# A linear recurrent unit whose three products go by the seven-product scheme, and whose sqrt(1 - a^2) is made without a reciprocal

## The reference, cut to what matters

```python
h = rms_norm(x, mix_norm[0])
u = h @ w_in                                   # [512, 1024] @ [1024, 2048]
gate_branch, x_branch = jnp.split(u, 2, axis=-1)
gate_branch = jax.nn.gelu(gate_branch)
xc = causal_depthwise_conv(x_branch, conv_w, conv_b)        # width 4
r = sigmoid(xb @ w_r + b_r); i = sigmoid(xb @ w_i + b_i)    # 16 blocks of 64 x 64
log_a = 8.0 * r * log_sigmoid(lam)
a = exp(log_a)
bt = sqrt(-expm1(2.0 * log_a)) * (i * xc)
hs[t] = a[t] * hs[t - 1] + bt[t]               # scan over the tokens
x = x + (gate_branch * hs) @ w_out             # @ [1024, 1024]
```

## Time and profile before

| | us |
|---|---|
| median of 3 runs | 3106.22 (3105.04 to 3106.98) |
| the profiled execution | 3106.63 |
| its span, first to last instruction | 3104.9 |
| TensorE busy | 3003.0 (97%) |
| VectorE busy | 1768.4 (57%) |
| ScalarE busy | 649.4 (21%) |
| Pool busy | 412.3 (13%) |
| recurrent unit, first product matmul to the MLP's first | 34.15 to 228.50 |

### The profile page before, as it was taken

How to read it: one execution, slowest core, us unless ns; L and a number is a source line. 1 busy time by engine, 2 the same in 40 slices (tenths; PEclk the granted TensorE clock), 3 DMA queues, 4 the chain that set the end, 5 groups by cost and what they waited for, 6 DMA issues and landing times.

```text
span 3104.9 us, 42252 instructions
## 1 busy us (share of the span) xinstructions
PE 3003.0 (97%) x18102; PEld 2554.3 (82%) x18102; DVE 1768.4 (57%) x2317; ACT 649.4 (21%) x1184; POOL 412.3 (13%) x390
## 2 busy tenths in 40 slices
PE   6989999999899999989989999999999999999998
PEld 5878888888678888878778878888888777888887
DVE  4646645455454653531566668887556134877754
ACT  1311100021341110002336531221010164111201
POOL 2112210120001220020013301111120011111101
PEclk9999999999999999999999999999999999999999
DMA  4222231322102222212100022223222100222320
GB/s 120 68 66 83 82 109 55 96 69 68 41 14 83 94 82 77 87 56 69 61 1 4 4 91 82 82 82 102 75 82 82 55 1 19 68 92 94 102 75 28
DMA packets 207574, 209.50 MB, mean 67 GB/s; under 512 B 8996, under 2 KB 206332, under 8 KB 207388
## 3 DMA queue, kind: packets, MB, share of 16 engines
q1 hardware_dynamic: 207356, 206.76, 20.9%
q10 hardware_dynamic: 32, 0.03, 0.0%
HBM read 204.65 MB, written 2.10 MB: 67 GB/s over the span
## 4 chain that ended last, share of the span: by engine, by line
PE 91%; DVE 5%; ACT 2%; issue 1%; POOL 1%; SPq 1%; DMA 0%; POOLq 0%; DVEq 0%; ACTq 0%
PE pp L252 55%; PE pp L149 16%; PE pp L1179 4%; PE pp L2626 2%; PE pp L2606 1%; PE pp L1915 1%; PE pp L1284 1%; PE pp L1898 1%; PE pp L1574 1%; PE pp L1870 1%; PE pp L2655 1%; PE pp L1307 1%; PE pp L2278 1%; DVE arena L328 1%; DVE arena L1015 1%
## 5 line engine op out<-in xcount | busy, mean ns | idle before, releaser
L252 PE MATMUL pp<-arena 128*128 128x264 f32 (+1 forms) x8176 | 1800.6, 383 | 5.9 <-DVE arena L309 4.1
L252 PEld LDWEIGHTS pp<-arena 128*128 128x128 f32 x8176 | 1550.3, 190 | 254.8 <-DVE arena L309 5.5
L149 PE MATMUL pp<-arena 128*128 128x256 f32 (+5 forms) x2400 | 536.4, 384 | 10.7 <-DVE arena L1025 8.0
L149 PEld LDWEIGHTS pp<-arena 128*128 128x128 f32 (+4 forms) x2400 | 447.2, 187 | 96.0 <-issue 15.6
L810 POOL TENSOR_TENSOR sq<-sq 128x512 f32<-128x512 f32 (+1 forms) x48 | 80.6, 1680 | 741.9 <-ACT sq L790 739.0
L340 ACT COPY arena<-pp 128x528 f32<-128x528 f32 (+1 forms) x58 | 33.6, 580 | 584.4 <-PE pp L252 539.4
L328 DVE TENSOR_TENSOR arena<-arena 128x256 f32<-128x256 f32 (+4 forms) x172 | 145.6, 869 | 6.0 <-POOL arena L2507 2.4
L2433 ACT ACTIVATE arena<-arena,par 128x528 f32<-128x528 f32 x88 | 68.1, 821 | 385.8 <-DVE arena L2464 385.8
L2507 POOL TENSOR_TENSOR arena<-arena 128x528 f32<-128x528 f32 x44 | 72.1, 1638 | 494.5 <-DVE arena L2476 494.5
L1149 POOL TENSOR_TENSOR arena<-arena 128x1024 f32<-128x1024 f32 x32 | 83.4, 2607 | 324.8 <-ACT arena L1097 281.6
L1179 PE MATMUL pp<-arena 128*128 128x256 f32 (+1 forms) x576 | 125.7, 380 | 0.0
(11 more groups left out here) (290 smaller groups left out, 2830.1 us busy)
## 6 DMA issues: line engine op xcount, KB each, us to landing
arena<-in_mlp_w_dram SPq DMA_DIRECT2D x64, 1024.0 KB, 5.5
arena<-in_ffn_up_dram SPq DMA_DIRECT2D x44, 1024.0 KB, 5.1
arena<-in_ffn_down_dram SPq DMA_DIRECT2D x16, 1408.0 KB, 8.0
arena<-in_fox_w_in_dram SPq DMA_DIRECT2D x12, 1024.0 KB, 5.5
arena<-in_lru_w_in_dram SPq DMA_DIRECT2D x8, 1024.0 KB, 7.0
arena<-in_lru_w_out_dram SPq DMA_DIRECT2D x4, 1024.0 KB, 5.2
arena<-in_fox_w_out_dram SPq DMA_DIRECT2D x4, 1024.0 KB, 5.3
arena<-in_rw_wk_dram SPq DMA_DIRECT2D x4, 1024.0 KB, 7.6
```

Source lines behind the costliest of these rows:

```text
L149: mm = pe.matmul(bank[0:m, h, 0:r.shape[1]], slot[0:kp, kk, j * P:j * P + m], r, start=kt == 0, stop=kt == nk - 1)
L252: return pe.matmul(k.pp[seventh(k, name, n, i) % NB][:, j, 0:hw], stationary[i][:, kk, j * P:(j + 1) * P], moving[i][:, kk, :], start=kk = ...
```

## The change

Three things, all in `stage_lru`:

1. The x, gate and output products use `plan_seven` and `product_seven`. VectorE gets their weight sums, input sums and `combine`; ScalarE gets six `keep_first` copies. `first_sums` of the x product is run by the stage ahead (`stage_scale`, now with `late=True`, which moves the root of the norm behind the first copy). For x and gate, `combine` stores through `stored`: one add out of PSUM and one multiply by `rs` for each output quarter of two tiles.
2. 1 - a^2 is tanh(-log a) times (1 + a^2). ScalarE makes a^2 with a second exponential (scale `c16`) into xc, once Pool has read xc; VectorE does one fused operation, `root_square`. The add and the reciprocal go.
3. The order on VectorE is new, since outputs now come in groups of four tiles: convolutions 0 to 3 behind the first pair of the x product, 4 to 7 behind the second; scans 0 to 3 behind the first pair of the gate product, 4 to 7 behind the second; then y with the output product's input sums.

The semaphores of weight and input sums are shared by all stages with counting bases (`Steps`, `weight_steps`, `input_steps`), which changes no order.

```diff
-    plan_product(k, "lru_x", w_in, [(D, 2 * D)], "dve")
+    norm = plan_seven(k, "lru_x", w_in, [(D + c1, D + c2) for c1, c2 in PAIRS])
     k.psum.add("lru_ri", ["act"] * (2 * KT))
-    plan_product(k, "lru_gate", w_in, [(0, D)], "dve")
-    plan_product(k, "lru_out", w_out, [(0, D)], "dve")
+    plan_seven(k, "lru_gate", w_in, PAIRS)
+    plan_seven(k, "lru_out", w_out, [(2 * n * GW + GW, 2 * n * GW) for n in range(2)])
...
+    def first_sums(e):
+        e.wait_ge(k.h_ready, hb + KT)
+        weight_sums(e, k, "lru_x", 0, Sx, xsum_s, "a21")
+        input_sums(e, X, T_, 0, KH, hw, hin_s, 0, (0, 1))
+        weight_sums(e, k, "lru_x", 0, Sx, xsum_s, "s2")
+        weight_sums(e, k, "lru_x", 0, Sx, xsum_s, 1)
+        input_sums(e, X, T_, 0, KH, hw, hin_s, 0, (2, 3))
...
     def act(e):
+        keep_first(e, k, "lru_x", 0, tx, hw)
+        root(e, k, norm)
...
         for f in range(KT):
             e.activation(T[:, f, :], r[:, f, :], ACT.Tanh, scale=nc8[:, f:f + 1]).then_inc(ta, 1)
-            e.wait_ge(ta, 2 * f + 1)
+            e.wait_ge(ix_s, f + 1)
+            e.activation(xc[:, f, :], r[:, f, :], ACT.Exp, scale=c16[:, f:f + 1]).then_inc(ta, 1)
+            e.wait_ge(ta, 3 * f + 2)
             e.activation(r[:, f, :], r[:, f, :], ACT.Exp, scale=c8[:, f:f + 1]).then_inc(ta, 1)
+        was_read(e, k, seventh(k, "lru_x", 1, THREE))
+        e.wait_ge(conv, KT)
+        keep_first(e, k, "lru_gate", 0, to, hw)
         for f in range(KT):
+            if f == KT // 2:
+                keep_first(e, k, "lru_gate", 1, to, hw)
             e.wait_ge(m2_s, f + 1)
             e.activation(T[:, f, :], T[:, f, :], ACT.Sqrt).then_inc(ms_s, 1)
...
     def dve(e):
...
+        for n in range(2):
+            add = stored(lambda f, half: xb[:, f:f + 2, 3 + half * hw:3 + (half + 1) * hw], n, x_s)
+            combine(e, k, "lru_x", n, tx, ux, hw, add,
+                    middle=(lambda e: weight_sums(e, k, "lru_x", 1, Sx, xsum_s, 0)) if n == 0 else None)
+            if n == 0:
+                weight_sums(e, k, "lru_x", 1, Sx, xsum_s, 1)
+            for f in range(4 * n, 4 * n + 4):
+                convolve(f)
...
+        for f in range(4):
+            root_square(f)
+        combine(e, k, "lru_gate", 0, to, uo, hw, stored(gate_at, 0, g_s),
+                middle=lambda e: weight_sums(e, k, "lru_gate", 1, S_, gsum_s, 0))
+        weight_sums(e, k, "lru_gate", 1, S_, gsum_s, 1)
+        for f in range(4, KT):
+            root_square(f)
+        for f in range(4):
+            scan(f)
+        combine(e, k, "lru_gate", 1, to, uo, hw, stored(gate_at, 1, g_s))
+        for f in range(4, KT):
+            scan(f)
         for f in range(KT):
             e.wait_ge(gelu, f + 1)
             e.tensor_tensor(gate[:, f, :], gate[:, f, :], xc[:, f, :], ALU.mult).then_inc(y_s, 1)
-        residual_lru(e)
+            if f % 2:
+                e.wait_ge(y_s, f + 1)
+                input_sums(e, gate, T_, f // 2, f // 2 + 1, hw, oin_s, 4 * (f // 2))
+        for part in range(2):
+            weight_sums(e, k, "lru_out", 0, S_, osum_s, part)
...
-    upto("lru", lambda: stage_scale(k, ["mix_norm0"], META), lambda: stage_lru(k))
+    upto("lru", lambda: stage_scale(k, ["mix_norm0"], META, late=True), lambda: stage_lru(k))
```

161 lines of the change are left out of this document (108 added, 53 removed).

## The result

The changed kernel takes 3117.19 us (median of 11 runs, 3111.67 to 3119.47), the kernel before 3106.22 (11 runs beside it, 3103.04 to 3107.11): a ratio of 1.0031, 95% interval 1.0023 to 1.0039. It is slower by 11 us, as forecast. Its profiled execution took 3113.33 us (span 3111.6); it is one of the four fastest of its eleven runs, 3.9 us under their median.

A forecast was written before the change was run, and what follows sets the result against it. TensorE, busy 97% of the span, was taken as the bound, with new waits eating its 20.7 us saving. Stretches -1.4 + 7.3 - 2.1 + 0.5 + 1.5 = +5.8 us, clock +5: +11, 3117 us; eight in ten 3106 to 3124.

The forecast's parts named there:

- x product: Up to the gate matrices: waits of 1.5 and 3.85 us; 6.9 us saved, 5.4 given back, 1.4 shorter.
- Gate matrices: Late convolutions of tiles 4 to 7, slowed 0.95 us per Pool multiply: stretch of 21.1 us, 7.3 more.
- Gate product: TensorE waits 5.0 us for ScalarE's copy of ONE behind 24 activations; stretch 53.4 us, 2.1 shorter.
- Output product: 10.1 us until its first matmul, then waits for sums; from gate product's end 66.65 us, 0.5 longer.
- MLP: Way into the MLP: last two tiles of x finished together, a wait before FOUR, 1.5 us longer.
- Clock: Low clock behind the new waits: 1.2, 1.0, 1.9 and 0.9 us, together +5, between 0 and 8.
- A: Gate matrices: Pool and VectorE don't delay each other, short waits leave the clock alone; 3106 or 3108; chance 0.14.
- C: Gate matrices: each Pool multiply holds VectorE for its whole instruction; 2.2 us more, 3121; chance 0.12.
- B: Pool and VectorE locks as in the forecast's sum, but the clock never falls; +5.8 us, 3112; chance 0.12.
- D: TensorE's work decides: with half the new waits gone 3103 or 3100, with none left 3086; chance 0.08.

The follow-up runs named there:

- e1_again: The changed kernel run again with no edit: 3117.5 us, ratio 1.0035 to the kernel before; span 3116.3.
- after: The first profiled execution of the changed kernel, no further edit: 3113.33 us, span 3111.6.
- e10: Kernel before with the new formula, scans ahead of the gate scaling, and the output product alone by seven: 3092.78 us, ratio 0.996.
- e2: Changed kernel with Pool's multiplications only after the last convolution: 3111.19 us, ratio 1.0016 to the kernel before.
- e3: Changed kernel with ScalarE's copy of the gate product's ONE after tile 3's activations, not tile 7's: 3107.44 us, ratio 1.0002 to the kernel before.
- e5: Kernel before with the new formula alone, all three products plain: 3105.27 us, ratio 1.0.
- e7: Changed kernel with the old formula back (addition, reciprocal and doubled product on VectorE): 3136.12 us, ratio 1.01 to the kernel before.
- e6: Kernel before with the new formula, and each scan ahead of its tile's gate scaling: 3097.11 us, ratio 0.9973.
- e11: Changed kernel with x product plain, early copy of ONE, scans 4 to 7 in the combining, first four y earlier: 3100.25 us, ratio 0.9984 to before.
- e4: Changed kernel with the output product plain, as in the kernel before: 3114.22 us, ratio 1.0028 to the kernel before.
- e9: Changed kernel with the x product plain, convolved tile by tile under it: 3112.03 us, ratio 1.0021 to the kernel before.
- e8: Changed kernel with late Pool multiplications, early copy of ONE, and scans 4 to 7 inside the second pair's combining: 3101.37 us, ratio 0.9984 to before.

## Why the prediction was right

The forecast was 3117, the measurement is 3117.19. The mechanism holds: every wait that was forecast came, ended by what was forecast. That the two figures agree within a microsecond is luck in part. Against the traces the gate matrices were put 1.9 us too long (their clock term included). In e1_again that is made up by 0.6 us more in the gate product, 0.9 more from there to the attention's squares and 0.9 in the rest of the program, which was put at nothing; in the profile of after nothing makes up for it, the last two fall short of the forecast as well (0.7 and 1.5), and it stays 4 us under. Step by step:

- *x product.* Waits of 1.5 and 3.85 us were forecast before SIX and FOUR; they are 1.00 (and 0.25 before SEVEN) and 3.16. The last weight sum ended at 49.6 (forecast 49.8) and TWO was read at 56.5 (57.1), but the last tile of h was there at 41.51, 0.4 us before the row that I started from. The clock took more than its 1.2: 160 records in 36.50 us, 1.8 over the free 34.70 of e10. From the last tile of h the stretch is 51.4 us; the forecast had 49.8 and 1.2.
- *Gate matrices.* 7.3 us more was forecast, 6.4 measured. The convolutions of tiles 4 to 7 end at 99.1, 104.6, 107.4 and 111.2; the forecast, moved by the 1.2 us of low clock ahead of it, had 98.9, 104.6, 107.4 and 112.2. Tile 7 met one Pool multiplication in full, not two. The price of one (0.95 forecast) is 0.88 to 0.90. The clock's 1.0 us for this stretch did not show: what TensorE did slowly there lay under VectorE. e2 confirms the cause: without Pool's part the stretch is 5.4 us shorter, and the kernel 6.3 by the medians.
- *Gate product.* The wait before FOUR is 4.89 us, 5.0 forecast, ended by ScalarE's copy, and 160 records take 36.42 us: 1.7 of clock, 1.9 forecast. e3 confirms that it is the copy's place alone: the wait and the low clock behind it go.
- *Output product.* 10.21 us (10.1 forecast) to the first matmul, then the first weight sum ended at 190.7 and SEVEN's wait with it, 22.3 us after the gate product's end (168.4; 22.65 forecast). SIX never waited for the last one by itself. The second SIX wait is 2.23 (2.35 forecast).
- *MLP.* 0.99 us of wait where 1.5 was forecast. 0.7 us more go there, at full clock: 0.3 of it in the 32 records before the wait, which take 7.37 us (from 243.77) where 32 records take 7.07 in the earlier trace rows. What slows them stays open.
- *Clock.* The term was +5 between 0 and 8. The profile of after shows 1.8 and 1.7 us of it, 3.5 in all, and e1_again 2.3 more in these stretches: 5.8. It is the term that was least sure, and the runs of the changed kernel themselves spread over it: four of the eleven lie at 3111.7 to 3113.3 with a mean granted clock of 0.988 to 0.989, seven at 3116.3 to 3119.5 with 0.985 to 0.987. The profiled execution belongs to the first, so the traces account for 6.7 us of the 11, and e1_again's for all of it.

Of the rivals, A falls by the rows of the convolutions and by e2, and C by the same rows: Pool's multiplications of 1.27 to 1.36 us cost 0.9 each, less than their length. The Trainium skill, page "SBUF — State Buffer", sections "SBUF: two separate sides" and "Who interferes with whom", says that a VectorE instruction with two SBUF inputs and a GpSimd one that reads SBUF exclude each other, and that whichever starts first holds the shared ports for its whole instruction. Taken as a delay of 1.27 us for each multiplication, that is too high a price by these rows. B, a clock that never falls, is excluded by the 36.50 and 36.42 us. Its figure, 3112, is where the fastest runs of the changed kernel lie, but that is no support for it: the profile of one of them holds 3.5 us of low clock. D falls: all the waits came.

One sentence of the forecast was too modest. It cost the missing reciprocals at nothing because they "lay beside TensorE's work"; in the kernel before that is so (e5), but in the changed kernel they would cost 19 us (e7). The sum was not touched by it, since they are absent from both sides of it, but the sentence hid what the new formula is there for.

What e6, e10 and e11 add: the change put the scheme where its sums come late. Alone on the output product, behind a gate product that leaves VectorE time, it keeps 4.3 us of its 6.9 (3097.1 to 3092.8). In the changed kernel the same scheme at the same place gains nothing: it loses 3.3 by the medians, 0.6 by the trace of after (e4). On the x product it loses 5.5 (e9), more than half of it through Pool's multiplications, which fall beside the late convolutions.

## What to carry to other kernels

A scheme that trades TensorE's work for another engine's paid here only where that engine had finished its share before TensorE wanted it; so look in the timeline at what the helper engine does in the stretch ahead, and convert first the product whose predecessor leaves it idle. Taking work off an engine brings nothing until the order of its instructions is changed to use the time, and the order nothing until there is time: here each was worth 0 us (the order as far as it could be had alone) and both together about 9. And lay out the waits of a new order by hand from the rows of a stage that is written the same way: six waits were forecast within 0.7 us like this.

## What the runs showed of the hardware that was not expected

- The same wait can be followed by a low clock or not. Behind the second SIX wait of 2.2 us the 96 records took 20.99 us (granted clock 1.00) in after, e2, e3, e10 and e11, and 22.64 to 22.68 (0.65 and 0.78 in the first two windows of e1_again) in e1_again, e7, e8 and e9. Behind every single wait of 3.16 us and more that was read (up to 14.48) the work took longer, but not by the same amount: behind the 3.16 us before FOUR of the x product the 160 records took from 36.20 us (e8) to 37.81 (e2), against 34.70 at full clock. Behind the 1.54 us of e6 it took no longer. What decides at 2.2 us wasn't found: the order of instructions and the waits ahead are the same in after and e1_again. The Trainium skill, page "TensorE: Matmul & The Clock Gate", Part 1, says that the chip's watch on TensorE's activity runs freely, so that the slow start of one and the same kernel differs from run to run; that would do for these waits in mid-kernel too, but no run here tests it.
- The copy moved early gained 10.1 us in the medians where its trace shows 6.7. Part of that is the clock in places that the edit doesn't touch, but why those runs have less of the low clock stays open.
- Pool's multiplications delay VectorE more than they are delayed: a VectorE operation of 0.54 us took 1.49 beside one of 1.27 us, 0.95 more. Pool's own take 1.27 us beside an idle VectorE (the kernel before, 99.19 us) and from 1.27 to 1.74 in after. Beside the weight sums and fused operations of e2 eight take 15.6 us, 0.68 more each, while the last three of the four weight sums take 2.2 to 2.3 us in place of 1.22 and the four fused operations 1.7 in place of 0.69.
